# Splitting the threshold counts of the sample group between VectorE and ScalarE, at three rounds for two projection units

## What is computed

```python
def sample_dsa(q, k, v, iq, ik, iw, ck, cv, cik, page_table):
    ...
    L = past + T
    n_sel = min(TOPK_MAX, L // 4)          # 256 of 8200
    ...
    sc = index_scores(iq, iw, ik_all, key_pos[None, :] <= q_pos[:, None])
    vals, idx = lax.top_k(sc, n_sel)
```

## Time and profile before

| | |
|---|---|
| median of 3 runs | 6124.88 us (6119.53 to 6135.17) |
| profiled execution, first to last instruction | 6036.5 us |
| median less that span | 88.4 us |
| mean granted clock of PE | 0.846 of full |
| busy: PE, PEld, DVE, ACT | 4906.7, 3128.4, 3171.2, 1310.5 us |
| front stage of the first layer | from the start to about 627 us |

### The profile page before, as it was taken

The page is one execution under the profiler, slowest core; times in us unless marked ns, Lnnn a source line. Parts: engine busy times, 40 slices in busy tenths (PEclk is TensorE's granted clock), DMA queues, the critical chain, the costliest instruction groups (busy, mean ns, idle before and its releaser), DMA issues. The chain is left out here.

```text
span 6036.5 us, 60851 instructions
## 1 busy us (share of the span) xinstructions
PE 4906.7 (81%) x22402; PEld 3128.4 (52%) x22402; DVE 3171.2 (53%) x7046; ACT 1310.5 (22%) x2564; POOL 298.4 (5%) x328
## 2 busy tenths in 40 slices
PE   5999575376687899999879986844867878999997
PEld 3344353244565488864343434533555655888543
DVE  2257565378774377740021666544787743777401
ACT  1210232046353100000022002311563521000000
POOL 1000231000000000000010003400000000000000
PEclk9999666576698999999989996655757989999998
DMA  8731442220002211122185324422100022111222
GB/s 288 228 111 62 121 122 61 53 59 16 10 24 94 109 65 61 57 87 66 58 290 182 117 68 127 130 51 58 29 16 20 16 107 101 64 64 58 92 66 100
DMA packets 377980, 529.78 MB, mean 88 GB/s; under 512 B 70690, under 2 KB 280548, under 8 KB 369028
## 3 DMA queue, kind: packets, MB, share of 16 engines
q1 hardware_dynamic: 347988, 391.68, 20.4%
q0 software_dynamic: 29696, 134.24, 6.9%
HBM read 382.17 MB, written 153.80 MB: 89 GB/s over the span
## 5 line engine op out<-in xcount | busy, mean ns | idle before, releaser
L447 PE MATMUL pp<-w_in,nT 128*128 128x512 f32 x1792 | 804.4, 601 | 0.0
L447 PEld LDWEIGHTS pp<-w_in,nT 128*128 128x128 f32 x1792 | 332.4, 192 | 393.4 <-issue 393.3
L3443 PE MATMUL x<-nT,wgu 128*128 128x272 f32 x2112 | 510.6, 395 | 15.3 <-DMA wgu<-in_w_gate 15.3
L3620 PE MATMUL pm<-w_down,hT 128*128 128x512 f32 x1024 | 448.3, 596 | 28.5 <-DMA hT<-scratch_hT 28.5
L3443 PEld LDWEIGHTS x<-nT,wgu 128*128 128x128 f32 x2112 | 404.4, 192 | 100.0 <-DMA wgu<-in_w_gate 15.9
L3443 PE MATMUL x<-n_sum,w_sum 128*128 128x272 f32 x1408 | 341.3, 396 | 12.7 <-DVE n_sum L3502 12.7
L3648 DVE TENSOR_TENSOR x_tile<-pm,x_tile 128x512 f32<-128x512 f32 x32 | 22.1, 692 | 611.0 <-PE pm L3620 611.0
L3620 PEld LDWEIGHTS pm<-w_down,hT 128*128 128x128 f32 x1024 | 195.8, 191 | 275.3 <-issue 275.3
L3526 DVE RECIPROCAL exp_neg<-one_more 128x544 f32<-128x544 f32 x88 | 312.7, 3554 | 3.0
L3443 PEld LDWEIGHTS x<-n_sum,w_sum 128*128 128x128 f32 x1408 | 270.1, 192 | 69.8 <-issue 13.5
L2626 POOL DMA_INDIRECT kv_sel<-in_cache_kv,kv_idx x256 | 247.2, 966 | 1195.2 <-DVE kv_idx L2769 992.5
(11 more groups left out here) (708 smaller groups left out, 8168.8 us busy)
## 6 DMA issues: line engine op xcount, KB each, us to landing
scratch_pages<-page_quarters POOLq DMA_DIRECT2D x32, 1024.0 KB, 9.1
area<-scratch_pages SPq DMA_DIRECT2D x64, 512.0 KB, 9.4
w_in<-in_w_in SPq DMA_DIRECT2D x14, 2048.0 KB, 8.9
scratch_hT<-hT SPq DMA_DIRECT2D x44, 544.0 KB, 2.9
wgu<-in_w_gate SPq DMA_DIRECT2D x22, 1024.0 KB, 5.4
wgu<-in_w_up SPq DMA_DIRECT2D x22, 1024.0 KB
hT<-scratch_hT SPq DMA_DIRECT2D x16, 1408.0 KB, 7.3
w_down<-in_w_down SPq DMA_DIRECT2D x16, 1024.0 KB
```

The source lines that it names most:

```text
L447: ins = pe.matmul(pp[u % 2][:, 0:cw], nT[:, k, t * P:(t + 1) * P], w[:, k, 0:cw], start=(k == 0), stop=(k == KT - 1))
L3443: ins = pe.matmul(out[:, j, :], left[:, k, :], right[:, k, j * QN:(j + 1) * QN], start=(k == 0), stop=(k == HK - 1))
L3620: ins = pe.matmul(pm[b][n][:, :], h[b][:, k, :], weights(k, slice(n * 512, (n + 1) * 512)), start=(k == 0), stop=(k == FT - 1))
```

## The change

The rounds get new places. Three rounds go into two units, after slices 5, 11 and 16 of the sixteen. In an odd unit (33, 35, ...) one round's total is taken after the unit's slice 5; in an even unit (34, 36, ...) one after its slice 3 and one after its slice 8, that is at its end. The 32 rounds run from unit 33 to unit 54 (round 31 after slice 3 of unit 54).

Each round's count is shared. DVE counts the first 2080 columns. ACT takes the other 2080 with one `Sign` activation, whose sum over the columns stands for the count; it waits for a new semaphore `cand_r`, counted up by the DVE instruction that makes the candidate. PE waits for both (`counted`, `signed`) and adds them with two tiny matmuls into one PSUM column, the second against `sign_pair`, which is `pair` times -0.5 and is made once.

On ACT, the step of a unit does its rounds' signs before the eviction, but the round at the unit's end after it.

Since a sum of signs takes a score equal to the candidate for half, DVE makes after the last round the next larger value (`next_above`, eight small operations), counts once more over all 4160 columns in its step of unit 54, PE adds that up after unit 55, and `settle_exactly` chooses between the two. The tables start in DVE's step of unit 56. SP's program, the end of PE's program and the tables themselves stay as they were. `zero` goes, and `page_ends` now lies in the tile `iq_all`.

```diff
+    SHARE = N // 2
+    ROUND_AT = (5, 11, 16)
+    def place_of(k):
+        two, n = divmod(k, len(ROUND_AT))
+        u, slice_end = divmod(KT * 2 * two + ROUND_AT[n], KT)
+        return (COUNT0 + u - 1, KT) if slice_end == 0 else (COUNT0 + u, slice_end)
...
+    EXACT = place_of(BITS)[0] + 1
+    TABLES = EXACT + 1
...
 # PE
+                    if u in rounds_at:
+                        k0 = 0
+                        for end, k in rounds_at[u]:
+                            slice_of(u, k0, end)
+                            add_counts(k)
+                            k0 = end
+                        if k0 < KT:
+                            slice_of(u, k0, KT)
+                        return
...
+                def add_counts(k):
+                    pe.wait_ge(counted, k + 1)
+                    pe.wait_ge(signed, k + 1)
+                    pe.matmul(ptot[:, k:k + 1], pair, cnt[:, k, 0:1], start=True, stop=False)
+                    pe.matmul(ptot[:, k:k + 1], sign_pair, cnt[:, k, 1:2], start=False, stop=True).then_inc(total, 1)
...
-                    k = u - COUNT0 - 1
-                    if 0 <= k <= BITS:
-                        pe.wait_ge(counted, k + 1)
-                        pe.matmul(ptot[:, k:k + 1], pair, cnt[:, k:k + 1], start=True, stop=True).then_inc(total, 1)
-                    elif k == BITS + 2:
+                    if u == EXACT:
+                        pe.wait_ge(counted, BITS + 2)
+                        pe.matmul(ptot[:, BITS + 1:BITS + 2], pair, cnt[:, BITS + 1, 0:1], start=True, stop=True).then_inc(total, 1)
+                    elif u == TABLES + 1:
                         pe.wait_ge(fin_c, 1)
...
 # ACT
+                def sign(k):
+                    act.wait_ge(cand_r, k + 1)
+                    act.activation(hit[:, N - SHARE:N], s[:, N - SHARE:N], ACT.Sign, bias=cand[:, 0:1].bitcast(F32), scale=-1.0, accum_out=cnt[:, k, 1:2]).then_inc(signed, 1)
...
+                    if u in rounds_at:
+                        last = [k for end, k in rounds_at[u] if end == KT]
+                        for end, k in rounds_at[u]:
+                            if end < KT:
+                                sign(k)
+                        evict(u)
+                        for k in last:
+                            sign(k)
+                        return
                     evict(u)
...
 # DVE
+                    dve.tensor_scalar(sign_pair, pair, -0.5, None, ALU.mult)
...
-                def count(k, value):
-                    dve.tensor_scalar(hit, s[:, :], value, 0.0, ALU.is_ge, ALU.add, accum_out=cnt[:, k:k + 1]).then_inc(counted, 1)
+                def count(k, n=N - SHARE):
+                    dve.tensor_scalar(hit[:, 0:n], s[:, 0:n], cand[:, :].bitcast(F32), 0.0, ALU.is_ge, ALU.add, accum_out=cnt[:, k, 0:1]).then_inc(counted, 1)
...
                         settle(k - 1)
-                        chain(dve.tensor_tensor(cand[:, :], thr[:, :], bit[:, k - 1:k], ALU.bitwise_xor))
-                        count(k, cand[:, :].bitcast(F32))
+                        dve.tensor_tensor(cand[:, :], thr[:, :], bit[:, k - 1:k], ALU.bitwise_xor).then_inc(cand_r, 1)
+                    dve.wait_ge(cand_r, k + 1)
+                    count(k)
...
+                    for _, k in rounds_at.get(u, ()):
+                        select(k)
                     if 2 <= u < NTURN + 2:
                         turn_out(u - 2)
-                    k = u - COUNT0
-                    if 0 <= k <= BITS:
-                        select(k)
-                    elif k == BITS + 1:
+                    if u == EXACT - 1:
+                        settle(BITS)
+                        next_above()
+                        count(BITS + 1, N)
+                    elif u == TABLES:
                         write_tables()
```

More of the change, by code:

```diff
@@ L186, in stage_front @@
     N = HALF + NS
+    SHARE = N // 2
+    HELD = 65535
+    ROUND_AT = (5, 11, 16)
[3 more added lines that the diff above has]
+        return (COUNT0 + u - 1, KT) if slice_end == 0 else (COUNT0 + u, slice_end)
+    rounds_at = {}
+    for k_ in range(BITS + 1):
+        u_, end_ = place_of(k_)
+        rounds_at.setdefault(u_, []).append((end_, k_))
+    EXACT = place_of(BITS)[0] + 1
+    TABLES = EXACT + 1
     def puts_on(b, n):
@@ L234, in stage_front @@
         keep = st.sb("keep", [P, 1], I32)
-        zero = st.sb("zero", [P, 1])
         one = st.sb("one", [P, 1])
-        cnt = st.sb("counts", [P, BITS + 1])
+        cnt = st.sb("counts", [P, BITS + 2, 2])
+        turn = st.sb("sign_of_thr", [P, 1], I32)
+        part = st.sb("thr_parts", [P, 4], I32)
         fin = st.sb("above_equal", [P, 2])
         lim = st.sb("limits", [P, 5])
-        ends = st.sb("page_ends", [P, NPAGES // 2 + 1])
+        ends = qa[:, 0, 0, 0:NPAGES // 2 + 1]
         pp = [st.ps(f"pp{i}", [P, 512]) for i in range(2)]
@@ L246, in stage_front @@
         pi = [st.ps(f"pi{i}", [P, 512])[:, :] for i in range(2)] + [pt[i][:, :, :].rearrange("p a n -> p (a n)") for i in range(2)]
-        ptot, pfin = acc[:, 0:BITS + 1], acc[:, 64:72]
+        ptot, pfin = acc[:, 0:BITS + 2], acc[:, 64:72]
+        sign_pair = xn[0][:, 0:P]
         ident, masks = const["ident"], const["masks"]
@@ L260, in stage_front @@
         got = [st.sem(f"got{n}") for n in range(RING)]
-        (counted, total, fin_c, fin_p, ranked, rank_p, ends_r, table_r, out_stored) = (st.sem(n) for n in (
-            "counted", "total", "final_counted", "final_total", "ranked", "rank_total", "ends_ready", "table_ready", "table_stored"))
+        (cand_r, counted, signed, total, fin_c, fin_p, ranked, rank_p, ends_r, table_r, out_stored) = (st.sem(n) for n in (
+            "cand_ready", "counted", "signed", "total", "final_counted", "final_total", "ranked", "rank_total", "ends_ready", "table_ready", "table_stored"))
         with nc.Block() as block:
@@ L683, in piece @@
                         place(J // GROUP - 1)
-                def count(k, value):
-                    dve.tensor_scalar(hit, s[:, :], value, 0.0, ALU.is_ge, ALU.add, accum_out=cnt[:, k:k + 1]).then_inc(counted, 1)
+                def count(k, n=N - SHARE):
+                    dve.tensor_scalar(hit[:, 0:n], s[:, 0:n], cand[:, :].bitcast(F32), 0.0, ALU.is_ge, ALU.add, accum_out=cnt[:, k, 0:1]).then_inc(counted, 1)
                 def settle(k):
+                    enough = TOPK - 0.5 - SHARE
@@ L690, in settle @@
                     dve.wait_ge(total, k + 1)
                     if k == 0:
-                        chain(dve.tensor_scalar(thr[:, :], ptot[:, 0:1], TOPK - 0.5, -1.0, ALU.is_lt, ALU.mult))
+                        chain(dve.tensor_scalar(thr[:, :], ptot[:, k:k + 1], enough, -1.0, ALU.is_lt, ALU.mult))
+                        dve.tensor_copy(turn[:, :], thr[:, :])
                     else:
-                        chain(dve.scalar_tensor_tensor(out=keep[:, :], in0=ptot[:, k:k + 1], scalar=TOPK - 0.5, in1=bit_f[:, k - 1:k], op0=ALU.is_ge, op1=ALU.mult))
+                        chain(dve.scalar_tensor_tensor(out=keep[:, :], in0=ptot[:, k:k + 1], scalar=enough, in1=bit_f[:, k - 1:k], op0=ALU.is_ge, op1=ALU.mult))
@@ L695, in settle, with next_above @@
                         chain(dve.tensor_tensor(thr[:, :], thr[:, :], keep[:, :], ALU.bitwise_xor))
+                def next_above():
+                    low, high, carry, least = (part[:, i:i + 1] for i in range(4))
+                    chain(dve.tensor_tensor(cand[:, :], thr[:, :], turn[:, :], ALU.bitwise_xor))
+                    dve.tensor_scalar(high, cand[:, :], -(HELD + 1), None, ALU.bitwise_and)
+                    chain(dve.tensor_scalar(low, cand[:, :], HELD, None, ALU.bitwise_and))
+                    dve.tensor_scalar(carry, low, HELD - 0.5, HELD + 1.0, ALU.is_ge, ALU.mult)
+                    chain(dve.tensor_scalar(least, low, 1.0, None, ALU.add))
+                    chain(dve.tensor_scalar(least, least, HELD, None, ALU.bitwise_and))
+                    chain(dve.tensor_tensor(high, high, carry, ALU.add))
+                    chain(dve.tensor_tensor(cand[:, :], high, least, ALU.bitwise_xor))
+                    chain(dve.tensor_tensor(cand[:, :], cand[:, :], turn[:, :], ALU.bitwise_xor))
@@ new lines, in settle_exactly @@
+                def settle_exactly():
+                    dve.wait_ge(total, BITS + 2)
+                    chain(dve.tensor_scalar(keep[:, :], ptot[:, BITS + 1:BITS + 2], TOPK - 0.5, -1.0, ALU.is_ge, ALU.mult))
+                    chain(dve.tensor_tensor(cand[:, :], cand[:, :], thr[:, :], ALU.bitwise_xor))
+                    chain(dve.tensor_tensor(cand[:, :], cand[:, :], keep[:, :], ALU.bitwise_and))
+                    chain(dve.tensor_tensor(thr[:, :], thr[:, :], cand[:, :], ALU.bitwise_xor))
@@ L701, in select @@
                         chain(dve.tensor_tensor(s[0:NS, HALF:], s[0:NS, HALF:], masks[0:NS, CAUSAL_QK8, 0:NS], ALU.add))
-                        count(0, zero[:, 0:1])
```

(11 more changed lines are left out.)

## The result

On the chip of the first comparison the changed kernel took 6254.8 us (6246.0 to 6265.7, 4 runs) against 6127.4 for the kernel before: ratio 1.0206, 95% interval 1.0189 to 1.0224, 127 us slower. The range was 6201 to 6272 and the forecast 6240, so the time lies between the forecast and the rival in which the clock falls behind nearly every wait (6263).

The account below looks back on a forecast made before the run. PE's own matmul stream was taken to bound the counting rounds; 7.6 + 2.8 + 30.8 + 10.7 - 9.3 = 42.6 us a layer, 85 for two, plus 30 for clock falls, gave 6240 us, range 6201 to 6272.

Parts of the forecast that it names:

- the rival in which the clock falls behind nearly every wait: Front stage's counting rounds: 14 clock falls a layer at 1.9 us each, giving 6263 us; chance 0.22.
- What bounds the stage: Middle of the counting rounds: PE's matmuls set the time; DVE's 4.55 us count hides under 6.87 us, except at sample units.
- The durations: Each round: half count on DVE 2.38 us, sign sum on ACT 2.10, two tiny matmuls 0.45; exact count hidden.
- The wait at an even unit's end: PE waits for a sign that ACT's program places behind that unit's eviction: 3.05 us, ten places a layer, 30.8 us.
- The sum without the clock: Front stage: tiny matmuls and new waits less old losses, 42.6 us a layer, 85 for two.
- the old fall: Unit 36 before the change: PE fell to mostly 1.2 GHz after a wait, costing 1.9 us a layer.
- irregular waits: Seven rounds in units 34 and 36 and around sample units 45 and 54: 10.7 us a layer together.
- the 9.3 us of old waits and fall: Old losses a layer at sample units 36, 45, 54, 63: 3 x 1.7 + 1.7 + 2.5; the most the change returns.
- The end of the stage: After unit 71: the tables' nine-unit head start gains 0, at most 0.3 us a layer.
- The step that was mis-sized is the clock: PE's clock behind the new waits: eight falls a layer at 1.9 us, 15 us, 30 for two layers.
- a little over half: Share of ten unit-end waits and four longest irregular ones expected to drop PE's clock: eight a layer.
- a sign of being wrong: PE at 1.2 GHz for more than one short stretch behind each wait, putting the time over 6272 us.

Follow-up runs that it names:

- the filler kernel: Changed kernel plus three unread PE matmuls before the total at each even unit's end; 6135.3 us, 1.0159 of the kernel before.
- The late start: Changed kernel with all signs ahead of evictions, first round in unit 38 instead of 33, tables from unit 61; 6054.8 us, 1.0030 of the kernel before.
- the early tables: The late start with PE's two tiny matmuls after unit 68 and SP's page counts and ranks after unit 69's store; 6017.2 us, 0.9974 of before.
- the last two kernels: The early tables, 6017.2 us; and the same with count and sign sum through one two-column tiny matmul, 6007.5 us, 0.9951 of the kernel before.
- the changed kernel's other profile: Changed kernel, nothing altered, run again on another chip; 6179.2 us, 1.0226 of the kernel before.

## Why the prediction was right, and where it was off

**What bounds the stage.** Right. With nearly all of PE's waits gone the counting stretch is 274.1 us, 0.9 more than before, with DVE's count halved; halving it bought nothing by itself.

**The durations.** The half count took 2.38 us (2.38), the sign 2.02 with its sum read 2.11 after the start (2.10), the pair of tiny matmuls 0.44 to 0.45, the exact count was hidden.

**The wait at an even unit's end.** Right in place and size: 3.05 us forecast; PE idle 2.87 us in the row, and 3.10 by the pairs, which has in it that the weight load too starts only behind the wait (at 425.65). Undoing it alone took 4.79 us from a steady pair (20.40 to 15.61), of which 20.40 - 18.71 = 1.69 is the clock by the filler kernel and 3.10 the wait.

**The sum without the clock.** 42.6 us a layer with the old fall counted as given back, 44.5 without it. The filler kernel, nearly free of falls, shows 43.9. Its irregular waits came out somewhat under the forecast: PE was idle 1.65, 2.91, 0.81, 0.75 and 1.42 us in rounds 1, 4, 7, 18 and 31, where 2.3, 3.5, 1.2, 0.9 and 1.7 stand in the sum, 0.16 of each for more than the wait's length. The late start shows that the 9.3 us of old waits and fall are indeed given back.

**The end of the stage.** Right: 16.99 us before and after. That PE's and SP's programs were the reason is shown by the early tables.

**The step that was mis-sized is the clock.** I took eight falls a layer at 1.9 us, 15 us. There were eleven low stretches and 54.6 us at 1.2 GHz, which is 25.6 us of lost work more than before. The term came out at 66.4 - 43.9 = 22.5 us a layer; the filler kernel puts the net price of the falls that it removes at 19 us a layer. That the net is less than the lost work fits a wait that is missing where PE was slow: the filler kernel has PE idle 0.75 us in unit 45, the changed kernel, at 1.2 GHz there, has none. The price of a fall was about right (a low stretch of 3.4 us cost a steady pair 1.69 us, for 1.9); two other things were too low. Nearly every end wait drew a fall, for the steady pairs at the same point each time (PEclk 0.66 in 426 to 431 and again in 447 to 452). And a fall was not always one short stretch: at sample unit 36, with a wait before its half-width matmuls' end and one behind them, the clock stayed low for 13.7 us, and behind units 38 and 44 for 6.8. I had named more than one short stretch behind each wait as a sign of being wrong, with a time over 6272; it was so at three places of eleven, and the time stayed under. In direction the rule of the Trainium skill ("TensorE: Matmul & The Clock Gate", section "Why this matters for your kernels"), no long idle gaps between bursts, was the better guide than my "a little over half", and this trace agrees with it in the main: eight end waits in a row, units 38 to 52, drew a fall each, while that of unit 34, as long, drew none. The rival built on that gave 6263, for 6254.8 measured.

**Faster was excluded for the right reason,** as neither the tables nor DVE was the bound; but the same idea, once SP's and PE's order let it through, is what makes the last two kernels faster than before.

## What to carry to other kernels

Before you move work to an idle engine, read that engine's own program order at the place: if what it must deliver stands behind something that waits for the receiver, the receiver pays for both, and here that one order cost more (50 us a layer) than all the rest of the change. The 2.87 us waits of a busy TensorE cost twice here, 3.10 us a pair of units as time and 1.69 as clock, and a filler shows which is which. A head start is worth something only when every program behind it, the queue that issues transfers too, lets the result go out early.

## What the runs showed of the hardware that was not expected

- At sample unit 36, which has a wait within it and one behind it, the clock was low for 13.7 us on end, where most waits between full units drew 3.4. In the changed kernel's other profile this was so in the second layer; in the first it was 6.8, then 3.4 at full speed, then 3.4 low. That the half-width matmuls are the cause is not shown.
- PE's idle 1.65 and 1.42 us in units 34 and 54 drew a fall, 2.87 us behind unit 34 drew none.
- Matmuls that do nothing useful made the counting stretch 16 to 19 us a layer shorter, since PE stayed at 2.4 GHz behind the end waits.
- The same stage with the same instructions took 392 us in one profile and 443 in another, most likely on unlike chips; kernels should be compared on one chip, and profiles by stretches that hold only what was changed.
